# Sparse attention loop: the probabilities are scaled before they are transposed, on three engines, and one bank collects all branches

## The reference, cut to what matters

```
p_c = _masked_softmax(s_c, d_c >= 0)                 # 31 compressed keys
o_c = einsum('ghqn,ngd->qghd', p_c, vc)
p_s = _masked_softmax(s_s, m_s[:, None])             # selected blocks
o_s = einsum('ghqk,gqkd->qghd', p_s, v_sel)
p_w = _masked_softmax(s_w, m_w)                      # window of 512
o_w = einsum('ghqk,kgd->qghd', p_w, vw)
o = g[..., 0:1] * o_c + g[..., 1:2] * o_s + g[..., 2:3] * o_w
```

## Time and profile before

| what | value |
|---|---|
| median of 3 runs | 3489.71 us (3489.36 to 3490.66) |
| the profiled execution's own time | 3483.9 us |
| its span | 3482.2 us |
| busy: PE / DVE / ACT / POOL | 3398.7 / 2411.0 / 1472.3 / 1065.8 us |
| mean granted TensorE clock | 0.993 of full speed |

### The profile page before, as it was taken

One profiled execution on the slowest core, in us unless ns is written; L12 is line 12 of the kernel. 1 busy time (PEld: TensorE's weight loads), 2 busy tenths in 40 slices (PEclk: granted clock), 3 DMA queues, 4 the chain that ended last, 5 costly groups with the idle time before them and its releaser, 6 DMA issues. The chain is left out here.

```text
span 3482.2 us, 56148 instructions
## 1 busy us (share of the span) xinstructions
PE 3398.7 (98%) x21983; PEld 2867.9 (82%) x21983; DVE 2411.0 (69%) x3238; ACT 1472.3 (42%) x2096; POOL 1065.8 (31%) x687
## 2 busy tenths in 40 slices
PE   8999999999999999999999999999999999999998
PEld 6889988645889978997777789988998888878997
DVE  6687774466777777786567587778777534468786
ACT  5644442465444453333544343344333422244333
POOL 1243322010243235443024045524542100015452
PEclk9999999999999999999999999999999999999999
DMA  3333334100223223333200133322322222213331
GB/s 122 97 101 106 103 105 97 37 1 13 97 98 106 99 85 98 108 101 98 64 26 8 57 103 104 108 85 97 110 96 97 85 85 85 85 58 103 107 101 69
DMA packets 232580, 296.26 MB, mean 85 GB/s; under 512 B 21893, under 2 KB 201464, under 8 KB 232392
## 3 DMA queue, kind: packets, MB, share of 16 engines
q1 hardware_dynamic: 230864, 290.48, 25.6%
q0 software_dynamic: 1152, 3.05, 0.4%
q10 hardware_dynamic: 376, 0.12, 0.0%
HBM read 291.53 MB, written 2.10 MB: 84 GB/s over the span
## 5 line engine op out<-in xcount | busy, mean ns | idle before, releaser
L337 DVE TENSOR_TENSOR wlo<-raw,whi 128x2048 fp32r<-128x2048 f32 x266 | 660.3, 2482 | 278.2 <-ACT whi L331 249.2
L331 ACT ACTIVATE whi<-raw 128x2048 fp32r<-128x2048 f32 x178 | 340.8, 1915 | 639.7 <-PE bank L343 549.2
L341 PE MATMUL bank<-u_hi,whi 128*128 128x512 f32 x1440 | 563.3, 391 | 4.2 <-DVE arena L3498 2.4
L343 PE MATMUL bank<-u_hi,wlo 128*128 128x512 f32 x1440 | 561.5, 390 | 0.0
L342 PE MATMUL bank<-u_lo,whi 128*128 128x512 f32 x1440 | 560.9, 389 | 0.0
L341 PE MATMUL bank<-h_hi,whi 128*128 128x512 f32 (+1 forms) x1340 | 536.0, 400 | 22.2 <-DVE h_lo L1136 9.9
L343 PE MATMUL bank<-h_hi,wlo 128*128 128x512 f32 (+1 forms) x1340 | 522.1, 390 | 0.0
L342 PE MATMUL bank<-h_lo,whi 128*128 128x512 f32 (+1 forms) x1340 | 522.1, 390 | 0.0
L509 PE MATMUL bank<-th,whi 128*128 128x256 f32 x1408 | 394.5, 280 | 2.3 <-DVE tmp L745 2.3
L511 PE MATMUL bank<-th,wlo 128*128 128x256 f32 x1408 | 392.8, 279 | 0.0
L510 PE MATMUL bank<-th,whi 128*128 128x256 f32 x1408 | 392.8, 279 | 0.0
(11 more groups left out here) (494 smaller groups left out, 6377.3 us busy)
## 6 DMA issues: line engine op xcount, KB each, us to landing
raw<-in_ffn_wgu SPq DMA_DIRECT2D x88, 1024.0 KB, 5.1
raw<-in_ffn_wd SPq DMA_DIRECT2D x44, 1024.0 KB, 4.8
raw<-in_mlp_w_up SPq DMA_DIRECT2D x32, 1024.0 KB, 5.3
raw<-in_mlp_w_down SPq DMA_DIRECT2D x32, 1024.0 KB, 4.8
raw<-in_odd_w_in SPq DMA_DIRECT2D x24, 1024.0 KB, 5.1
raw<-in_even_w_in SPq DMA_DIRECT2D x13, 1024.0 KB, 5.3
raw<-in_rg_w_in SPq DMA_DIRECT2D x8, 1024.0 KB, 5.3
raw<-in_odd_w_out SPq DMA_DIRECT2D x8, 1024.0 KB, 5.0
```

The costliest lines, as they stand in the source:

```text
L331: e.activation(whi[:, n % 2, :], raw[:, n % 2, :], ACT.Copy).then_inc(hi_ready, 1)
L337: e.tensor_tensor(wlo[:, n % 2, :], raw[:, n % 2, :], whi[:, n % 2, :].bitcast(F32), ALU.subtract).then_inc(lo_ready, 1)
L341: pe.matmul(o, w_hi, r_hi, start=first, stop=False)
L343: return pe.matmul(o, w_lo, r_hi, start=False, stop=last)
```

## The change

The softmax weights are applied to the probabilities before they are turned. `weigh(n, q)` is now made per query tile on VectorE: a reciprocal of two sums, and an instruction that limits and multiplies with the gates into `wq`. Then each tile is multiplied in place with its column of `wq`: head one's tiles 0 to 2 on GpSimd (`scale_p`), its tile 3 on ScalarE (`scale_a`), head two's four tiles on VectorE (`scale_b`). With that `spread`, `take_spread`, `combine`, `pick`, `osum` and `oadd` go. All branches of a pair accumulate in one PSUM bank, 5 or 6 by the parity of the pair, `values_cmp` too. Bank 7 joins the score ring, which has four banks from step 1 on. `turn_small` and `take_small` are made once a pair, in the other pair's output bank, and so wait for `o_lo`. The third copy of head two moves from ScalarE to VectorE, and ScalarE takes the first two copies of head one ahead of the exponentials. The subtraction of the compressed maxima and the scaling into `mt` move to GpSimd, and its biases are made between these.

```diff
+            b_ = v_ % 3 if key[0] == 0 else (7, 0, 1, 2)[(v_ - 10) % 4]
...
+            def scale_p(n):
+                for q in range(3):
+                    part = prob[n % 2][0][:, Q_AT[q]:Q_AT[q] + (q + 1) * P]
+                    e.wait_ge(wq_dve, 4 * n + q + 1)
+                    e.tensor_scalar(part, part, wq[:, n % 2, 2 * q:2 * q + 1], None, ALU.mult).then_inc(np_scaled, 1)
+            for j in range(PAIRS):
+                scale_p(2 * j)
+                e.wait_ge(cx_dve, j + 1)
+                e.tensor_tensor(flat, flat, cmx.unsqueeze(2).broadcast_to([P, 8, NC]), ALU.subtract).then_inc(cx_pool, 1)
+                scale_p(2 * j + 1)
+                e.wait_ge(cq_dve, j + 1)
+                if j:
+                    e.wait_ge(mt_pe, j)
+                for hd in range(2):
+                    ins = e.tensor_tensor(mt[:, :, 32 * hd:32 * hd + NC], cs[:, hd, :, 0:NC],
+                                          csum[:, 4 * hd:4 * hd + 4].unsqueeze(2).broadcast_to([P, QT, NC]), ALU.mult)
+                ins.then_inc(mt_pool, 1)
+                if j + 2 < PAIRS:
+                    biases(j + 2)
...
-                                pe.wait_ge(ex_act, 8 * n + 2 * q + hd + 1)
+                                if hd:
+                                    pe.wait_ge(nb_scaled, 4 * n + q + 1)
+                                elif q < 3:
+                                    pe.wait_ge(np_scaled, 3 * n + q + 1)
+                                else:
+                                    pe.wait_ge(na_scaled, n + 1)
...
+            def turn_small(j):
+                pe.wait_ge(mt_pool, j + 1)
+                if j:
+                    pe.wait_ge(o_lo, j)
                 for q in range(QT):
+                    ins = pe.transpose(pbank[5 + (j + 1) % 2][0:VR, q * P:q * P + P], mt[:, q, :], ident[:, :])
...
+            def values_cmp(j):
+                pe.wait_ge(ms_act, j + 1)
+                pe.matmul(pbank[5 + j % 2][:, :], vcbd[:, j // 4, :], ms[0:VR, :], start=False, stop=False)\
+                    .then_inc(cv_pe, 1)
...
-                    if i == 0 and n >= 2:
-                        spread(n - 2)
+                    if i == 1 and n % 2 == 0:
+                        turn_small(n // 2 - 1)
+                    if n >= 2 and i == (1 if n <= STEPS else 0):
                         values(n - 2, 2)
-                    if i == 1 and (n, "o") in unit_no:
-                        values_cmp(n)
                     if i and 1 <= n <= STEPS:
                         turn(n - 1, i - 1)
                         if i >= 2:
                             values(n - 1, i - 2)
-                        if i == 2:
-                            turn_small(n - 1)
+                        if i == 2 and n % 2 == 0:
+                            values_cmp(n // 2 - 1)
...
+            def scale_a(n):
+                part = prob[n % 2][0][:, Q_AT[3]:Q_AT[3] + S]
+                e.wait_ge(wq_dve, 4 * n + 4)
+                e.activation(part, part, ACT.Copy, scale=wq[:, n % 2, 6:7]).then_inc(na_scaled, 1)
...
+                    if i in (1, 2) and n <= STEPS:
+                        take_turned(n - 1, i - 1)
                     if n < STEPS:
                         exps(n, i)
+                    if i == 3 and n <= STEPS:
+                        take_turned(n - 1, 2)
...
+                    if i == 3 and n < STEPS:
+                        scale_a(n)
...
+            def weigh(n, q):
+                w = wq[:, n % 2, 2 * q:2 * q + 2]
+                e.wait_ge(ex_act, 8 * n + 2 * q + 2)
+                chain(e.reciprocal(w, sums[:, n % 2, 2 * q:2 * q + 2]))
+                e.scalar_tensor_tensor(w, w, 1e30, gates_of(n, 1 + n % 2)[:, q, :], ALU.min, ALU.mult).then_inc(wq_dve, 1)
+
+            def scale_b(n, q):
+                part = prob[n % 2][1][:, Q_AT[q]:Q_AT[q] + (q + 1) * P]
+                e.wait_ge(wq_dve, 4 * n + q + 1)
+                e.tensor_scalar(part, part, wq[:, n % 2, 2 * q + 1:2 * q + 2], None, ALU.mult).then_inc(nb_scaled, 1)
...
                         take_turned(n - 1, i - 1)
-                    if i == 1 and n >= 2:
-                        combine(n - 2)
+                    if i in (1, 2) and n < STEPS:
+                        weigh(n, i - 1)
+                        scale_b(n, i - 1)
+                    if i == 2 and n < STEPS:
+                        if n % 2:
+                            weigh_cmp(n - 1)
+                        weigh(n, 2)
                     if i == 3:
+                        if n < STEPS:
+                            scale_b(n, 2)
+                        if 1 <= n <= STEPS:
+                            take_turned(n - 1, 2)
+                        if n < STEPS:
+                            if (n, "c", 0) in unit_no:
+                                masked_cmp(n)
+                            weigh(n, 3)
+                            scale_b(n, 3)
+                            if (n, "c", 0) in unit_no:
+                                shift_cmp(n)
+                    if i == 3 and n >= 3 and n % 2:
+                        j = (n - 3) // 2
+                        e.wait_ge(o_hi, j + 1)
+                        e.tensor_tensor(rg_low(j), pbank[5 + j % 2][:, :], rg_high(j).bitcast(F32), ALU.subtract)\
+                            .then_inc(o_lo, 1)
```

More of the change, by code:

```diff
@@ L1726, in build @@
         unit_no = {}
-        for n_ in range(STEPS + 1):
-            keys = [(n_, q_, hd_) for q_ in range(QT) for hd_ in range(2)] if n_ < STEPS else []
+        for n_ in range(STEPS):
+            keys = [(n_, q_, hd_) for q_ in range(QT) for hd_ in range(2)]
             if n_ % 2 == 0:
-                keys[4:4] = [(n_, "o")] if n_ else []
-                keys += [(n_, "c", 0), (n_, "c", 1)] if n_ < STEPS else []
+                keys += [(n_, "c", 0), (n_, "c", 1)]
             for key in keys:
                 unit_no[key] = len(unit_no)
+        unit_bank, bank_before, last_in = [], [], {}
+        for key, v_ in unit_no.items():
+            b_ = v_ % 3 if key[0] == 0 else (7, 0, 1, 2)[(v_ - 10) % 4]
+            unit_bank.append(b_)
+            bank_before.append(last_in.get(b_))
+            last_in[b_] = v_
         def head_of(n, hd):
@@ L1779, in pool_nsa, with biases @@
             chain(e.memset(gz[:, :, NC:NC + 1], 0.0))
[L1780 to L1785, removed]
+            def biases(j):
                 if j == 1:
@@ L1843, in free_bank @@
             def free_bank(v):
+                for u in (v - 1, v):
+                    if bank_before[u] is not None:
+                        last = bank_before[u]
                 if v >= 3:
-                    pe.wait_ge(sc_dve, v - 2)
+                    pe.wait_ge(sc_dve, last + 1)
             def scores(n, q):
@@ L1928, in values @@
                 pe.wait_ge(pa_act, 3 * n + g + 1)
[L1929 to L1934, removed]
+                pe.wait_ge(pb_dve, 3 * n + g + 1)
+                if g == 0 and n % 2 == 0 and j:
+                    pe.wait_ge(ms_act, j)
                 for k in GROUPS[g]:
@@ L2028, in act_nsa @@
                         exps(0, m)
+                    scale_a(0)
                 if 1 < c < 9:
@@ L2089, in act_nsa @@
-                    if i and 1 <= n <= STEPS:
-                        if i == 3:
-                            take_small(n - 1)
-                        take_turned(n - 1, i - 1, 0, pa_act)
-                        if i == 3:
-                            take_turned(n - 1, 2, 1, pb_act)
-                            if n == STEPS:
-                                act_hi(e, n0 + 11)
-                    if i == 2 and n >= 3 and n % 2:
+                    if i == 3 and n <= STEPS:
+                        take_turned(n - 1, 2)
+                        if n == STEPS:
+                            act_hi(e, n0 + 11)
@@ L2098, in act_nsa @@
+                    if i == 3 and n < STEPS:
+                        scale_a(n)
+                    if i == 1 and n % 2 == 0:
+                        take_small(n // 2 - 1)
+                    if i == 1 and n % 2 and n < STEPS:
+                        e.wait_ge(cx_pool, n // 2 + 1)
+                        e.activation(cs[:, :, :, 0:NC], cs[:, :, :, 0:NC], ACT.Exp).then_inc(cx_act, 1)
+                    if i == 1 and n >= 3 and n % 2:
                         j = (n - 3) // 2
-                        e.wait_ge(o_sum, j + 1)
```

128 lines of the change are left out of this document (35 added, 93 removed).

## The result

The changed kernel took 3462.79 us (median of six runs, 3459.36 to 3467.54) against 3489.53 of the kernel before (3487.99 to 3493.3): a ratio of 0.9924, 95% interval 0.9911 to 0.9936.

The account below looks back on a forecast made before the run. A ring of hand-overs, with no engine full, was taken to bound the loop. Six pairs gain 6.0 us, the seventh 2.2, the ends 2.0, together 10.2: 3473.7, or 3479.5 as a median; range 3474 to 3485, wider 3465 to 3499.

Parts of the forecast that it names:

- The ring: Attention loop: PE's 9.9 us after rg_low in series with VectorE's 12.0, so 21.9 us a pair against 24.6.
- What stands in the way: End of odd steps: GpSimd and VectorE meet at the same operands, adding 0.5 and 1.2 us: 23.6 a pair.
- smaller meetings: GpSimd's mt with scale_b(2), and its second scaling with weigh_cmp, hold VectorE: 0.5 us a pair.
- one hold: Odd step: weigh gets in first, so only scale_b(3) is held, by one bias instruction, about 1.2 us.
- rival (2): Odd step: weigh and scale_b(3) are held by one bias each, 2.9 us; gain eaten, 3489.7; 20%.
- Rival (1): Odd step: no hold, as weigh slips in ahead and one-input scalings aren't held, or GpSimd's timing differs; 3468.8; 20%.
- Rival (3): GpSimd wins races for wq_dve, so scale_b(0) and scale_b(1) wait for instructions of 0.4 and 0.8 us; 3500.9; 15%.
- I give the clock no term: Loop pairs: granted clock priced at nothing, as one pair at 0.93 took 24.66 us and one at 1.00 24.60.
- VectorE's work: VectorE per pair: from 16.3 us, with instructions taken out and others added, to 19.0.
- the ends of the loop: Two spreads less in the tail and an earlier turn(0) at the start: 2.0 us gained (0 to 3).
- Adding 5.8 to the sum: Whole program: the runs' median lay above the profiled execution, so 5.8 us were added, 3473.7 becoming 3479.5.
- ScalarE's work: ScalarE stays below 15.5 us a pair; its cost is nothing, hidden under VectorE's 19, otherwise at most 0.72 a step.

Follow-up runs that it names:

- the probe: A small program of its own, without the attention: VectorE instructions alone and beside one- or two-input GpSimd instructions; longest hold 0.43 or 0.44 us against 1.05 to 1.09.
- the first two executions: The first profiled executions of the kernel before and the changed kernel, nothing else changed: 3483.9 and 3467.5 us.
- the second two: The kernel before and the changed kernel, unaltered, each profiled a second time: 3490.63 and 3464.71 us.

## Why the prediction was wrong

*The ring was right.* PE waited for rg_low as foreseen. The forecast had 9.9 us of PE from rg_low's end to scores_cmp, and 12.0 of VectorE in series. In the full-clock pair turn_small starts at 738.93, and the next masked_cmp at 748.64: 9.71. From masked_cmp at 727.10 to turn_small 11.83, with 0.3 of hold in it. The ring without a hold is 21.24 (no biases), against 21.9.

*The step that failed is "What stands in the way": the size of a hold.* The meeting came where I put it, but its price was 0.3 us a pair and not 1.7 (1.2 for one bias and 0.5 for smaller meetings). That the forecast took one hold and not two was luck, as the bias won the race in all six pairs: with the price that it used, its own schedule would have given the 3489.7 of rival (2), 26.9 above the measured time. I had taken the duration from a two-input GpSimd instruction and charged it to one-input ones; the probe has 1.05 to 1.09 and at most 0.44 for the two. In all that makes 6 x 1.7 less 5 x 0.3 = 8.7 us. Rival (1), no hold, 3468.8, came nearest, though not by its conditions: weigh did not slip in ahead, and a one-input scaling can be held, only briefly. Rival (2) had the order right and the price wrong: weigh's second instruction took 0.47 and not over 1. Rival (3) did not happen: no scale_b(0) took over 0.29 us.

*"I give the clock no term" is the second step that failed, and it was wrong twice.* It cost 1.58 us in each of four pairs of the changed kernel (23.11 against 21.53; 22.81 against 21.24 in the last), 6.3 in all; its half-rate piece is values(2) and turn(0), which stand in PE's part of the ring. And before it was not free: I had read one pair at 0.93 beside one at 1.00. Cut at masked_cmp, the first execution has 24.35 at 1.00 and 24.57, 25.11 and 25.58 at 0.93, so the price of a drop depends on where in the pair it falls.

*The sum.* The forecast's seven pairs are 6 x 23.6 + 22.4 = 164.0. Less 8.7 for the holds; less 1.7 for the first pair, which has no rg_low to wait for (20.23 against 21.9); less 4.0 for six rings of 21.24 instead of 21.9; less 0.5 for small meetings in the last; plus 6.3 for the clock: 155.4, where 155.45 was measured. VectorE's work was 1.3 a pair below my 19.0, but its serial part, which alone counts, was right to 0.5. So a term too high by 8.7 and one at nothing that was 6.3 partly cancelled. For the ends of the loop the forecast had 2.0; the last piece was 1.0 shorter in the first two executions (32.78 against 33.77) and 4.2 in the second two.

*The rest of the 26.7.* My forecast started from the first profiled execution, and 16.4 of gain is what that pair of executions shows, 6 more than the forecast. The other 10 are how the two executions happened to fall, 5.6 below the median for the kernel before and 4.8 above it for the changed one. Adding 5.8 to the sum took the first of these for a fixed distance. The second execution of the kernel before was longer by 1.8 us in the loop, with one pair at 0.87 and the last one at 0.93 instead of 1.00, and by 2.2 in the last piece, both in what was changed; the changed kernel's pairs took the same in both its executions. Two executions of each don't show whether that is the rule.

*What held.* PE waited for rg_low, as foreseen, and not for a copy; ScalarE's work stayed below 15.5 us a pair (14.5), though no run prices its extra scaling, or the loss of `combine` and `spread`, alone; the copies' new order is worth some 2 us, which is within the uncertainty. By parts, each taken from the changed kernel alone: fourth bank 37 us, scalings on GpSimd 13.5, order of copies 2. They don't add up to 26.7, and need not: each is the price in a kernel that has all the others, and holds what the clock took as well.

## What to carry to other kernels

Before an operation goes to GpSimd, price its meeting with VectorE from a row of the same kind of GpSimd instruction: one input or two makes a factor of two and a half in the longest hold here. When a loop is a ring of hand-overs, write down the last wait of the new ring; the cheapest next edit is to issue its releaser earlier (one block moved, 18 us). And read the clock's price from all the pairs cut at one event, not from one of each kind, because a wait of PE can cost twice: here 1.8 us for the wait itself and 1.6 for the slower matmuls behind it.

## What the runs showed of the hardware

- In the probe, a one-input GpSimd instruction in SBUF held one VectorE instruction for 0.44 us at most, a two-input one for 1.05 to 1.09, whatever the VectorE instruction was (one input of 512 elements, or two of 2). While a one-input GpSimd scaling of 1.56 us ran, VectorE's small two-input instructions were held once and then ran unheld.
- GpSimd's scaling of 128 x 512 took 1.56 us alone and 2.01 beside VectorE's scalings.
- PE idle for 2.16 us was followed by half-rate matmuls in some pairs (1.48 against 0.87 us for values(2)) and not in others with the same idle piece. With the piece filled, shortened to 0.7 us or removed, no pair behind the first fell below 1.00. But the kernel before, with no idle piece over 0.92 us in the loop, had pairs at 0.93 as well. What decides is open.
- A reordering of ScalarE alone moved the mean clock of the old loop's pairs from 0.93 and 1.00 to 0.82 to 0.93 and cost 17 us with no engine busier by more than 0.3 us a pair, except PE with its slower matmuls.
